# Sixteen modulation tiles in an earlier layer, a re-dealt beginning of the halved layers, and a convolution product one step on

## What is computed

```
m = silu(c) @ w_ada + b_ada               # six 1024-vectors a layer, from c for the image, c_ctx for the context
sh1, sc1, gt1, sh2, sc2, gt2 = split(m, 6)
x = x + gt1 * mixer(rmsnorm(x, g1) * (1 + sc1) + sh1)
h = rmsnorm(x, g2) * (1 + sc2) + sh2
x = x + gt2 * ((silu(gate) * up) @ w_down)      # layers 0, 1: gate, up = split(h @ w_in)
x = x + gt2 * ((silu(dwconv3(a)) * b) @ w_down) # layers 2, 3: a, b = split(h @ w_up); 2816 wide, 3 taps along the tokens
```

## Time and profile before

| | |
|---|---|
| median of 3 runs | 3387.64 us |
| the runs | 3385.45, 3387.64, 3387.78 us |
| profiled execution, its own time | 3385.83 us |
| its span, first to last instruction | 3384.5 us |
| instructions | 45127 |
| mean granted TensorE clock | 0.992 of full |
| TensorE busy | 3247.7 us |
| VectorE busy | 2159.3 us |
| ScalarE busy | 1404.8 us |
| weight refill high, ScalarE, x520 | 859 ns each |
| weight refill low, VectorE, x520 | 981 ns each |
| modulation tile, VectorE, x144 | 1235 ns each |

### The profile page before, as it was taken

One profiled execution on the slowest core, in us unless ns is written; L12 is line 12 of the kernel. 1 busy time (PEld: TensorE's weight loads), 2 busy tenths in 40 slices (PEclk: granted clock), 3 DMA queues, 4 the chain that ended last, 5 costly groups with the idle time before them and its releaser, 6 DMA issues. The chain is left out here.

```text
span 3384.5 us, 45127 instructions
## 1 busy us (share of the span) xinstructions
PE 3247.7 (96%) x17822; PEld 2767.8 (82%) x17822; DVE 2159.3 (64%) x3582; ACT 1404.8 (42%) x2261; POOL 223.0 (7%) x336
## 2 busy tenths in 40 slices
PE   6998999999999999999999999989999999999998
PEld 4787789999978888878888886889888987678887
DVE  4677477888765554558657466487888855654444
ACT  4567363333444334342223345363333443542333
POOL 0001100000010000003001000100000010010001
PEclk9999999999999999999999999999999999999999
DMA  5500123444221221215544211123444231123232
GB/s 216 216 23 2 38 77 123 132 143 137 87 90 50 96 77 50 90 69 195 173 148 156 84 45 51 44 86 116 140 127 129 87 99 57 44 83 99 90 101 83
DMA packets 98689, 334.39 MB, mean 99 GB/s; under 512 B 11872, under 2 KB 16768, under 8 KB 95024
## 3 DMA queue, kind: packets, MB, share of 16 engines
q1 hardware_dynamic: 77072, 252.63, 22.2%
q0 software_dynamic: 21408, 78.88, 7.4%
HBM read 329.37 MB, written 2.10 MB: 98 GB/s over the span
## 5 line engine op out<-in xcount | busy, mean ns | idle before, releaser
L1184 ACT ACTIVATE WH<-WR 128x1024 fp32r<-128x1024 f32 (+3 forms) x520 | 445.8, 859 | 1019.4 <-PE PS L586 749.1
L1797 DVE TENSOR_TENSOR WL<-WR,WH 128x1024 fp32r<-128x1024 f32 (+3 forms) x520 | 509.6, 981 | 478.6 <-ACT WH L1184 476.8
L586 PE MATMUL PS<-HH,WH 128*128 128x512 f32 (+1 forms) x1544 | 526.7, 373 | 10.7 <-DVE WL L1797 8.4
L586 PE MATMUL PS<-HH,WL 128*128 128x512 f32 (+1 forms) x1544 | 522.0, 370 | 0.0
L586 PE MATMUL PS<-HL,WH 128*128 128x512 f32 (+1 forms) x1544 | 521.7, 370 | 0.0
L586 PE MATMUL PS<-D,WH 128*128 128x512 f32 x1648 | 421.4, 361 | 0.3 <-DVE D L2244 0.2
L586 PEld LDWEIGHTS PS<-HH,WH 128*128 128x128 f32 x1544 | 270.0, 188 | 71.3 <-DVE WL L1797 12.9
L586 PEld LDWEIGHTS PS<-D,WH 128*128 128x128 f32 x1648 | 275.5, 188 | 52.5 <-DVE D L2244 2.0
L586 PEld LDWEIGHTS PS<-HL,WH 128*128 128x128 f32 x1544 | 268.9, 188 | 51.0 <-issue 1.0
L586 PEld LDWEIGHTS PS<-HH,WL 128*128 128x128 f32 x1544 | 269.2, 188 | 50.6
L586 PE MATMUL PS<-D,WL 128*128 128x512 f32 (+1 forms) x824 | 257.2, 360 | 0.0
(11 more groups left out here) (369 smaller groups left out, 6100.6 us busy)
## 6 DMA issues: line engine op xcount, KB each, us to landing
WR<-in_win SPq DMA_DIRECT2D x176, 512.0 KB, 3.5
AT<-in_adat POOLq DMA_DIRECT2D x144, 512.0 KB, 3.9
WR<-in_wret SPq DMA_DIRECT2D x64, 512.0 KB, 3.7
WR<-in_zin SPq DMA_DIRECT2D x36, 512.0 KB, 3.5
WR<-in_wdn SPq DMA_DIRECT2D x32, 448.0 KB, 3.4
WR<-in_wdn SPq DMA_DIRECT2D x48, 256.0 KB, 2.9
WR<-in_wdn SPq DMA_DIRECT2D x32, 320.0 KB, 2.9
AR<-in_ada SPq DMA_DIRECT2D x8, 1024.0 KB, 9.7
```

Of the source, the lines that this page charges most:

```text
L586: mm = PE.matmul(dst[:, a:b], w(u)[:, k * P:(k + 1) * P], h[:, k, a:b], start=(k == 0 and i == 0), stop=(k == nk - 1 and i == 2))
L1184: AC.activation(M.hi(u), M.raw(u), COPY).then_inc(*on.up("w_hi", u))
L1797: VE.tensor_tensor(M.lo(u), M.raw(u), M.hi(u).bitcast(F32), ALU.subtract).then_inc(*on.up("w_lo", u))
```

## The change

It has five parts.

- Layer 3's first 16 tiles (the wide ones) are dealt in layer 1's FFN and no longer in layer 2's. `ada_slots` is now asked for the FFN f in which tiles lie, and a tile is a pair (l, v). Layer 1's FFN holds 64 tiles: three in each up step with j < 4 of chunk 0 (`MORE`), two in the others, one in each down unit of chunks 0 and 1. Layer 2's holds 32 of one column: in its up steps at j = 4 of chunk 0, j = 0 of chunks 1 to 3 and all five of chunk 4, and in down units. In layer 0's, the tile of the third block moves to the fifth.
- A new tile X2, over the place of CB, holds the difference of `turned` n = 1 in place of XF's second part; `turned` n = 3 and the high and low of n = 1 read it there.
- The beginning is re-dealt. `turned(3)` moves from block 0 to q == 1 of the halves; two of block 2's weight sums to block 1 and q == 1; `turned_low` n = 1 stays in block 0, n = 2 comes in block 1 after the refills, n = 0 at q == 0, n = 3 at q == 3; ScalarE's `turned_high(0)` stands before a refill, `turned_high(3)` at q == 2.
- The convolution product: `conv_multiply(j-1)` moves from i == 2 to i == 5, and the `conv_high` and `conv_low` of that block to i == 1 of the next step (at i == 2 in the last).
- GpSimd's loads follow the new deal.

The diff, without the hunks that only rename what `ada_order` is asked for:

```diff
@@ -25,6 +25,8 @@
 WIDE_DOWN = (0, 4, 4, 3)
+EARLY = [(3, v) for v in range(16)]
+MORE = (4, 0, 0)
 H = 512
@@ -274,6 +276,8 @@
         self.TF = t("TF", [P, KT, T])
+        self.top = wide
+        self.X2 = t("X2", [P, 4, Q])
         self.top = wide
@@ -539,32 +543,45 @@
-def ada_slots(l):
+def ada_slots(f):
     at = {}
-    if l - 1 not in HALVED:
-        v = 0
-        for ch, nj in enumerate(CHUNKS[l - 1]):
+    wide, narrow = [(f + 1, v) for v in range(2 * KT)], [(f + 1, v) for v in range(2 * KT, NV)]
+    if f == 1:
+        wide = iter(wide + EARLY[:2 * KT])
+        narrow = iter(narrow + EARLY[2 * KT:])
+        for ch, nj in enumerate(CHUNKS[f]):
             for j in range(nj):
-                at["up", ch, j] = (v, v + 1)
-                v += 2
-            for m in range(NV - 2 * FT if ch == 0 else 0):
-                at["down", ch, m] = (v,)
-                v += 1
+                at["up", ch, j] = (next(wide), *(next(narrow) for _ in range(1 + (j < MORE[ch]))))
+            for m in range(KT if ch < 2 else 0):
+                at["down", ch, m] = (next(wide) if m < 5 else next(narrow),)
         return at
-    wide, narrow = iter(range(2 * KT)), iter(range(2 * KT, NV))
-    for ch, nj in enumerate(CHUNKS[l - 1]):
-        for j in range(3 if ch == 0 else 0, nj):
-            at["up", ch, j] = tuple(next(narrow) for _ in range(1 + (0 < ch < 4 and j in (1, 2))))
+    if f == 2:
+        narrow = [t for t in wide + narrow if t not in EARLY]
+    wide, narrow = iter(wide), iter(narrow)
+    for ch, nj in enumerate(CHUNKS[f]):
+        for j in range(nj):
+            if f == 0:
+                n = (2 if j == 4 else 0) if ch == 0 else 1 + (ch < 4 and j in (1, 2))
+            else:
+                n = int(j == 4 if ch == 0 else j == 0 or ch == 4)
+            tiles = tuple(t for t in (next(narrow, None) for _ in range(n)) if t)
+            if tiles:
+                at["up", ch, j] = tiles
         for m in range(0 if ch else 1, KT - 2 if ch < 4 else 0):
-            at["down", ch, m] = (next(wide if ch == 0 or m in (1, 3, 4, 5)[4 - WIDE_DOWN[ch]:] else narrow),)
+            if f == 0 and (ch == 0 or m in (1, 3, 4, 5)[4 - WIDE_DOWN[ch]:]):
+                at["down", ch, m] = (next(wide),)
+            else:
+                tile = next(narrow, None)
+                if tile:
+                    at["down", ch, m] = (tile,)
     return at
-def ada_order(l):
-
-    return list(sum(ada_slots(l).values(), ()))
+def ada_order(f):
+
+    return list(sum(ada_slots(f).values(), ()))
@@ -1325,7 +1342,7 @@
         else:
-            dst, src = M.XH[:, n], M.XF[:, n]
+            dst, src = M.XH[:, n], M.X2[:, :, :] if n == 1 else M.XF[:, n]
         AC.activation(dst, src, COPY).then_inc(*on.up("t_hi", (l, n)))
@@ -1377,15 +1394,19 @@
             j, i = order[q - 1] if q else (None, None)
+            if l > 0 and i == 1 and j > js[1]:
+                conv_high(j - 2)
             if i in (1, 5, 6) or i == 3 and l > 0:
                 keep(j, i)
+            if l > 0 and i == 2 and j == js[-1]:
+                conv_high(j - 1)
             if q == 0 and ch:
                 refill(ahead(2))
             if q + 3 < len(order):
                 refill(ahead(q + 3))
             if q == len(order) - 2 + len(order) % 2:
                 refill(FIRST["down", l, ch])
-            if ch == 0 and q == 1:
+            if ch == 0 and q == 2:
                 turned_high(l, 3)
@@ -1398,8 +1419,6 @@
             else:
-                if i == (4 if j == js[-1] else 5) and j > js[0]:
-                    conv_high(j - 1)
                 if i == 4:
@@ -1444,13 +1463,13 @@
                     whole(f"{l}b", l, [(1, k) for k in range(0 if l < 2 else 4, KT)])
+                    turned_high(l, 0)
                 refill(W.after(u, 4 if l in HALVED and jj else 3))
                 AC.wait_ge(*on("up_taken", (l, jj)))
                 AC.activation(M.DH[l][:, j, 0:n], HF[:, 0:n], COPY).then_inc(*on.up("d_hi", (l, jj)))
                 if l in HALVED and jj == 0:
                     turned_high(l, 1)
                     turned_high(l, 2)
-                    turned_high(l, 0)
             if l in HALVED:
@@ -1817,22 +1836,22 @@
-    def ada_tiles(l, tiles):
-
-        order = ada_order(l)
-        for v in tiles:
-            n = order.index(v)
+    def ada_tiles(f, tiles):
+
+        order = ada_order(f)
+        for l, v in tiles:
+            n = order.index((l, v))
             AT, cols = M.AT[n % 2], ada_columns(l, v)
             VE.wait_ge(*on(f"mod_load{n % 2}", (l, v)))
             if n:
-                VE.wait_ge(*on("ada_taken", (l, order[n - 1])))
+                VE.wait_ge(*on("ada_taken", order[n - 1]))
             for j in cols:
                 i = VE.scalar_tensor_tensor((AT if j == len(cols) - 1 else PS[3])[:, :], AT[:, :], 1.0, M.CB[:, j, :],
                                             ALU.mult, ALU.mult, accum_out=MOD[:, l, v, j:j + 1])
             i.then_inc(*on.up("ada_taken", (l, v)))
     def ada_bias(l):
-        VE.wait_ge(*on("ada_taken", (l, ada_order(l)[-1])))
+        VE.wait_ge(*on("ada_taken", ada_order(l - 1)[-1]))
         for j in range(2):
@@ -2044,9 +2063,9 @@
         VE.wait_ge(*on("h_whole", (tag, 1, 3 if n == 0 else KT - 1)))
-        dst, a, b = ((M.XF[:, 0], M.TF[:, 0:4, Q:T], M.TF[:, 0:4, 0:Q]), (M.XF[:, 1], M.TF[:, 4:8, Q:T], M.XF[:, 0]),
+        dst, a, b = ((M.XF[:, 0], M.TF[:, 0:4, Q:T], M.TF[:, 0:4, 0:Q]), (M.X2[:, :, :], M.TF[:, 4:8, Q:T], M.XF[:, 0]),
                      (M.XF[:, 2], M.TF[:, 4:8, Q:T], M.TF[:, 0:4, Q:T]),
-                     (M.TF[:, 4:8, 0:Q], M.TF[:, 4:8, 0:Q], M.XF[:, 1]))[n]
+                     (M.TF[:, 4:8, 0:Q], M.TF[:, 4:8, 0:Q], M.X2[:, :, :]))[n]
         if n in (1, 3):
@@ -2057,7 +2076,7 @@
         else:
-            dst, src, hi = M.XL[:, n], M.XF[:, n], M.XH[:, n]
+            dst, src, hi = M.XL[:, n], M.X2[:, :, :] if n == 1 else M.XF[:, n], M.XH[:, n]
         VE.tensor_tensor(dst, src, hi.bitcast(F32), ALU.subtract).then_inc(*on.up("t_lo", (l, n)))
@@ -2081,7 +2100,7 @@
         js, order, segs = range(plain(l, ch), nj), halves_order(l, ch), segments(l)
-        slots = ada_slots(ada)
+        slots = ada_slots(l)
@@ -2145,6 +2164,10 @@
             j, i = order[q - 1] if q else (None, None)
+            if l > 0 and i == 1 and j > js[1]:
+                conv_low(j - 2)
+            if l > 0 and i == 2 and j == js[-1]:
+                conv_low(j - 1)
             if i == 5:
@@ -2163,27 +2186,29 @@
                 refill(FIRST["down", l, ch])
+            if ch == 0 and q == 0:
+                turned_low(l, 0)
             if ch == 0 and q == 1:
+                turned(l, 3)
+            if ch == 0 and q == 3:
                 turned_low(l, 3)
             if l == 0:
                 if i in (6, 7) and j > js[0]:
                     low(j - 1, int(i == 6), i == 7)
             else:
-                if i == (4 if j == js[-1] else 5) and j > js[0]:
-                    conv_low(j - 1)
                 if i == 6 and j > js[0]:
                     conv(j - 1)
-                if i == 2 and j > js[0]:
+                if i == 5 and j > js[0]:
                     conv_multiply(j - 1)
-            if i == 1 and (ch or j > js[0]):
+            if i == 1:
                 weight_sum(up + 2 * j, 3)
             if (i == 2 and j > js[0] or i == 7 and j == js[0]) and j < js[-1]:
                 weight_sum(up + 2 * (j + 1), 5)
                 weight_sum(up + 2 * (j + 1), 6)
             if i == 1 and ("up", ch, j) in slots:
-                if ch == 0 and j == js[1]:
+                if ch == 0:
                     VE.wait_ge(*on("cb", ada))
-                ada_tiles(ada, slots["up", ch, j])
+                ada_tiles(l, slots["up", ch, j])
         j = js[-1]
@@ -2200,18 +2225,17 @@
         n = segs[-1][1]
-        slots = ada_slots(ada) if ada is not None else {}
+        slots = ada_slots(l) if ada is not None else {}
         for ch, nj in enumerate(CHUNKS[l]):
             up, first, c0 = FIRST["up", l, ch], FIRST["down", l, ch], start(l, ch)
             for j in range(plain(l, ch)):
                 jj, u, s = c0 + j, up + 2 * j, side(l, j, nj)
                 SG, HF = M.WK[2 * s], M.WK[2 * s + 1]
-                if l in HALVED and jj == 1:
-                    turned_low(l, 2)
-                    turned_low(l, 0)
                 refill(W.after(u, 2))
                 if l in HALVED and jj == 1:
                     refill(W.after(u, 3))
+                    turned_low(l, 2)
+                    weight_sum(up + 4, 7)
                 if l > 1:
@@ -2224,7 +2248,7 @@
                         VE.wait_ge(*on("cb", ada))
-                    ada_tiles(ada, slots["up", ch, j][:1])
+                    ada_tiles(l, slots["up", ch, j][:1])
                 if l in HALVED and jj == 0:
@@ -2239,16 +2263,15 @@
                         turned(l, 2)
-                        turned(l, 3)
```

(29 more changed lines are left out.)

6 lines of the change are left out of this document (3 added, 3 removed).

## The result

The changed kernel takes 3398.87 us (median of six runs, 3395.94 to 3399.89), the kernel before 3385.65 us in its six (3384.09 to 3387.78): ratio 1.0036, 95% interval 1.0024 to 1.0048. That is 13.2 us slower. It was forecast slower, at 3395.2 us, 7.6 us above before.

A forecast was written before the change was run, and what follows sets the result against it. TensorE, busy 96% of the span, bounds the kernel, so only its waits and low clock can be won. Terms -2.1 + 3.3 - 3.5 + 2.9 + 7.0 = +7.6 us gave 3395.2 us as median, range 3383 to 3402.

The forecast's parts named there:

- rival (c): Worse: clock falls in layer 2's 4.2 us stretch and squares hit three steps fully; +14, or 3402 us; chance 0.11.
- the five terms: Layer 0 beginning -2.1, layer 2 beginning +3.3, layer 2 chunks 1 to 3 -3.5, last chunk +2.9, second FFN +7.0 us.
- The replay of layer 2: Layer 2's beginning: (2,6) at 2247.1, (2,5) at 2253.65, nothing won there; +3.3 us by the chunk's last product.
- the 4.2 us wait: Layer 2's beginning: TensorE idle 4.2 us ahead of (2,6); if the clock falls, the stall before (2,5) covers it.
- the clock stays full at the beginning of layer 0: Sign of being right: no low clock at layer 0's beginning, where it had cost 1.5 us.
- the price of 0.4 us: Layer 0's beginning: CB loaded later, its Silu ahead of the refill of (3,2); 0.4 us off the 2.5 gained.
- VectorE now also waits for `conv_high`: Layer 2's steps: multiply, high, low, keep, refill follow directly; VectorE waits 0.9 us before every `conv_low`, `keep(j,1)` 1.0 later.
- The replay of chunk 1: Layer 2: stalls at (2,2), (2,3), (2,4) and before (3,4) go, (3,6) and down pair lose 1.2 each; gain 1.2 us.
- Rival (b): Faster: layer 2's stalls in chunks 1 to 3 vanish with the tiles; -13 us, or 3374.5; chance 0.12.
- Steps 0, 1 and 2: Second FFN, chunk 0, three tiles a step: TensorE loses 1.3, 1.1 and 2.0 us, the last with GpSimd's squares.
- Step 3: Second FFN, chunk 0: three tiles, two of them stretched by GpSimd's squares; 2.6 us lost.
- Rival (a): Squares or loads don't meet the three-tile steps; second FFN pays only its first two; +3 us, or 3390.6; chance 0.22.

The follow-up runs named there:

- conv_undone: The changed kernel with the convolution product (multiply, high, low) back where it was, tiles and beginning still changed: 3384.19 us, ratio 0.9992.
- squares_late: The changed kernel with GpSimd's eight context squares behind loads 24 to 31 of layer 1's FFN instead of 8 to 15: 3394.27 us, ratio 1.0025.
- keep_behind: On mixed: in layer 2, ScalarE's weight refill that follows product (j,1) stands ahead of keep(j,1): 3363.96 us, ratio 0.9941.
- mixed: Changed kernel, at most two tiles per up step in layer 1's FFN, re-dealt beginning in layer 0 only, convolution product where it was: 3372.32 us, ratio 0.9953.

## Why the prediction was right, and which terms were off

The direction and the range held: 3398.87 us lies in 3383 to 3402. The difference is 13.2 us where 7.6 were forecast, and the time lies as near to rival (c)'s 3402 as to the forecast's 3395.2. Each of the five terms has its sign right, and the steps behind them can be checked one by one. The sum has no time in it for a low clock behind the new waits, and that is the largest part of what is missing.

**Beginnings.** The replay of layer 2 was exact where it was done. The two traces are 2230.69 - 2220.13 = 10.56 us apart at the stretch's first row; 2257.67 - 10.56 = 2247.11 for (2,6), forecast 2247.1, and 2264.21 - 10.56 = 2253.65 for (2,5), forecast 2253.65. The clock did fall behind the 4.2 us wait (0.54 in the window below) and, as said, the wait before (2,5) covered it. For layer 0, (2,5) was forecast at 487.1: 488.50 in the trace, which began the stretch 1.36 later, so 487.14. The 2.5 us won up to there are exact too. The size was missed behind that point: in layer 2 +4.8 came instead of +3.3, because the moved convolution product costs 1.4 us in chunk 0 too, a term that the sum did not have. The re-deal alone, in the runs with the product where it was, costs 18.75 + 55.68 - 70.90 = 3.5, next to the forecast 3.3, though its bounds were wide. In layer 0 -0.8 came instead of -2.1: the statement "the clock stays full at the beginning of layer 0" was wrong. The new wait of 2.06 us before (2,5) was followed by the low clock (0.69), and that took 1.6 of the 2.5 us back. In the trace of conv_undone a wait of 2.13 us was not followed by it (1.00); there layer 0 gains 1.4 us (17.93 + 47.86 against 67.23). So the price of 0.4 us that the sum set behind (2,5) is 1.0 where the clock stays full, and the forecast -2.1 was too good in either case.

**Convolution product.** The step "VectorE now also waits for `conv_high`" is the mechanism, and its size, 0.9 us a step, is the trace's 0.92. `keep(j,1)` comes later only because the low part does: it starts right behind the low part in the kernel before too (at 2380.92 behind the low part of 2379.94 in chunk 1). The last chunk, +3.1, and chunks 1 to 3, -1.05 each, are near the forecast +2.9 and -1.2. The replay of chunk 1 had (3,6) right, with 1.39 us of stall where some 1.5 follow from it, the three stalls at (2,2), (2,3) and (2,4) gone, and 1.1 us lost in the down units. But (3,5), which was to wait as before (0.93), waits for nothing, and (3,4), whose wait was to go, waits 0.89 us as before. These two misses cancel, and that is luck. The forecast of chunks 1 to 3 hid two larger numbers of opposite sign, -4.2 for the tiles and +3.1 for the product. Rival (b) was right that the tiles' leaving frees stalls, two thirds of the 6.1 us, and wrong that the product's move leaves them free. (Half of the stalls gone, by its own sum, would be 3383.5 and not 3382.)

**Second FFN.** Steps 0, 1 and 2 were forecast at 1.3, 1.1 and 2.0 us and cost 1.8, 1.0 and 1.8. Step 3 was forecast at 2.6 and cost 4.0. TensorE's waits are 1.49, 0.75, 1.55 and 2.03 us and don't grow from 1 to 3, as was said they would. The mis-sized term is again the clock, 0.65 behind a wait of 2.03 us: 12 matmuls in 4 us instead of 18. The replay also stretched only the tiles, and not the refill of 1.74 us. Without the squares (squares_late) the four steps cost 4.4 us together, where 4.6 follows from the prediction's steps without its squares; with them 8.5. Rival (a) had it that the squares don't meet these steps; they do, and they carry half. The prediction sets one sentence of the section "The DRAIN you can't avoid" against the earlier trace rows; the section itself adds that a next instruction that is not held starts earlier, so rows of 1.14 us at a duration of 1.23 need not contradict the Trainium skill.

**Rival (c)**, 3402 us, had the clock falling behind the 4.2 us wait of layer 2. It fell there and cost nothing, as the forecast said. But its mechanism, a wait that brings the low clock with it, worked at (2,5) of layer 0 and in step 3 of the second FFN, some 1.6 us each, and with the 1.4 us of the moved product in chunk 0 that is most of what lifts the difference from 7.6 to the stages' 12.4.

## What to carry to other kernels

On an engine that limits a loop, look at what the neighbour must do between two of its instructions: put work between them that is due anyway. Keeping other work between a producer and its consumer was worth 13.8 us here, swapping two ScalarE instructions a further 6.7 (the stages of keep_behind against mixed), and both can be read off one step of the timeline as a gap of 0.9 or 1.1 us with the other engine's name behind it. Work that is moved to where an engine has room cost nothing here as long as no single step was filled beyond the other engine's length; beyond it a wait of 0.75 us cost 1.0, and one of 2.03 us cost 4.0 once the clock fell behind it. And when two parts of a change meet in one stage, price each alone: the sum here hid a gain of 4 under a loss of 3.
